# A block's output handed to the next block by single feature chunks, low halves one chunk behind

## The reference

```python
def rmsnorm(x, g):
    y = xf * lax.rsqrt(jnp.mean(xf * xf, axis=-1, keepdims=True) + RMS_EPS)
    return (y * g).astype(x.dtype)
# after each mixer and each network of the first block:
x = x + rmsnorm(y, g_post)          # y is the block's output
h = rmsnorm(x, g_pre)               # the next block's input
next_projection = h @ w             # 1024 features wide
```

## Time and profile before

| | us |
|---|---|
| median of 3 runs | 2015.49 |
| lowest and highest | 2012.11, 2020.97 |
| span of the profiled execution | 2011.9 |
| TensorE, VectorE, ScalarE, GpSimd busy in it | 1953.4, 1340.9, 1010.4, 320.4 |

### The profile page before, as it was taken

One profiled execution on the slowest core, in us unless ns is written; L12 is line 12 of the kernel. 1 busy time (PEld: TensorE's weight loads), 2 busy tenths in 40 slices (PEclk: granted clock), 3 DMA queues, 4 the chain that ended last, 5 costly groups with the idle time before them and its releaser, 6 DMA issues.

```text
span 2011.9 us, 34435 instructions
## 1 busy us (share of the span) xinstructions
PE 1953.4 (97%) x12338; PEld 1727.1 (86%) x12338; DVE 1340.9 (67%) x2732; ACT 1010.4 (50%) x1640; POOL 320.4 (16%) x138
## 2 busy tenths in 40 slices
PE   7998999999999999999999999999999999999998
PEld 6776787778778888999899999999999998888886
DVE  6357556656655558889787689933667766666666
ACT  5436546555554456666444455665444443333333
POOL 0000000000000000000000057877666600000000
PEclk9899999999989999999999999999999999999999
DMA  6242465533345553444343535555444455555554
GB/s 229 74 157 78 157 205 167 178 121 128 118 137 188 187 188 126 147 138 136 105 126 126 179 126 168 180 175 167 137 142 142 137 164 188 192 193 192 193 193 156
DMA packets 85150, 313.99 MB, mean 156 GB/s; under 512 B 9456, under 2 KB 9456, under 8 KB 84592
## 3 DMA queue, kind: packets, MB, share of 16 engines
q1 hardware_dynamic: 85040, 312.49, 46.6%
HBM read 311.40 MB, written 1.05 MB: 155 GB/s over the span
## 4 chain that ended last, share of the span: by engine, by line
issue 61%; PE 32%; POOL 6%; DVE 0%; POOLq 0%; DVEq 0%; ACT 0%
PE ps L414 17%; PE ps L282 12%; POOL wsplit L266 6%; PE ps L2642 3%; PE ps L430 0%; DVE work L2772 0%; DVE sq L2679 0%; POOLq L265 0%; PE ps L2718 0%; POOLq L2505 0%; DVE sq L2675 0%; DVE picks L2595 0%; PE ps L2608 0%; DVEq L2930 0%; DVE work L2687 0%
## 5 line engine op out<-in xcount | busy, mean ns | idle before, releaser
L260 ACT ACTIVATE wsplit<-ring 128x1024 fp32r<-128x1024 f32 x572 | 603.8, 1057 | 475.4 <-PE ps L414 270.4
L266 DVE TENSOR_TENSOR wsplit<-ring,wsplit 128x1024 fp32r<-128x1024 f32 x438 | 534.6, 1223 | 326.1 <-ACT wsplit L260 324.7
L282 PE MATMUL ps<-hsplit,wsplit 128*128 128x256 f32 x5064 | 646.2, 287 | 6.5 <-DVE hsplit L698 2.1
L282 PEld LDWEIGHTS ps<-hsplit,wsplit 128*128 128x128 f32 x5064 | 620.3, 193 | 14.3 <-issue 5.2
L266 POOL TENSOR_TENSOR wsplit<-ring,wsplit 128x1024 fp32r<-128x1024 f32 x134 | 320.2, 2396 | 1295.5 <-ACT wsplit L260 1295.5
L414 PE MATMUL ps<-wsplit,gsplit 128*128 128x512 f32 x1992 | 458.1, 391 | 0.0
L414 PEld LDWEIGHTS ps<-wsplit,gsplit 128*128 128x128 f32 x1992 | 374.4, 188 | 81.9 <-issue 4.2
L401 PE MATMUL ps<-wsplit,hsplit 128*128 128x512 f32 x1248 | 310.0, 406 | 17.2 <-DVE wsplit L266 10.6
L401 PEld LDWEIGHTS ps<-wsplit,hsplit 128*128 128x128 f32 x1248 | 241.9, 196 | 70.4 <-issue 18.9
L1783 PE MATMUL ps<-hsplit,wsplit 128*128 128x256 f32 x936 | 128.5, 289 | 0.0
L1783 PEld LDWEIGHTS ps<-hsplit,wsplit 128*128 128x128 f32 x936 | 116.3, 191 | 0.0
(11 more groups left out here) (318 smaller groups left out, 1698.5 us busy)
## 6 DMA issues: line engine op xcount, KB each, us to landing
ring<-in_weights SPq DMA_DIRECT2D x580, 512.0 KB, 3.3
work<-in_tables SPq DMA_DIRECT2D x1, 2123.0 KB, 12.5
xT<-in_x SPq DMA_DIRECT2D x1, 1024.0 KB, 4.9
work<-in_subkeys SPq DMA_DIRECT2D x1, 1024.0 KB, 15.2
work<-in_decay SPq DMA_DIRECT2D x2, 512.0 KB, 4.1
out_x<-work SPq DMA_DIRECT2D x2, 512.0 KB, 2.6
work<-in_w SPq DMA_DIRECT2D x1, 512.0 KB, 5.9
ring<-in_gain_row SPq DMA_DIRECT2D x1, 512.0 KB, 3.8
```

Of the source, the lines that this page charges most:

```text
L260: act.activation(wsplit[:, n % RING, 0, :], slab(s), ACT.Copy).then_inc(S("split", "lead"), 1)
L266: eng.tensor_tensor(wsplit[:, n % RING, 1, :], slab(s), wsplit[:, n % RING, 0, :], ALU.subtract).then_inc(S("split", RESTS[stream][0]), 1)
L282: mm = pe.matmul(dst, wsplit[:, n, a, c * P:(c + 1) * P], hsplit[:, b, c, :], start=(c == 0 and t == 0), stop=(c == KC - 1 and t == 2))
```

## The change

The three counters rise by one for each chunk. The add of every chunk signals, each leading half waits for its own chunk and signals, each low half waits for its own leading half and signals, and TensorE waits for one chunk's low half at a time. In the loop over chunks VectorE writes the low half of chunk c - 1 right behind the add of chunk c (before: a pair of low halves, one pair of adds behind), and the split of slab 1 stands behind the low half of chunk 1. `h_steps` works out the targets, since the inputs m0, m4 and m5 go on by pairs.

```diff
@@ split_project
             if pre is not None and c % 2 == 0:
-                wait_h_split(pe, pre, c // 2 + 1)
+                wait_h_split(pe, pre, c + 2)
@@
+    def h_steps(st, chunks):
+        whole = lambda s: KC if s[0] == "n" else KC // 2
+        return sum(whole(s) for s in HSPLITS[:HSPLITS.index(st)]) + (chunks if st[0] == "n" else chunks // 2)
@@ rest_h_vector
-        v.wait_ge(S("split", "h_lead"), HSPLITS.index(st) * 4 + c // 2 + 1)
+        v.wait_ge(S("split", "h_lead"), h_steps(st, c + 2))
@@
-    def wait_h_split(pe, st, steps=4):
-        pe.wait_ge(S("split", "h_rest"), HSPLITS.index(st) * 4 + steps)
+    def wait_h_split(pe, st, chunks=KC):
+        pe.wait_ge(S("split", "h_rest"), h_steps(st, chunks))
@@ split_columns
-        if pre is not None:
-            wait_h_split(pe, pre, q + 1)
         for cc in range(2):
             c = 2 * q + cc
+            if pre is not None:
+                wait_h_split(pe, pre, c + 1)
@@ ffn_tensor (moba_tensor and hgrn_tensor alike)
-        pe.wait_ge(S("norm", "x"), x_steps(POST[pre]) + 2)
+        pe.wait_ge(S("norm", "x"), x_steps(POST[pre]) + KC // 2)
@@ x_steps
-        return ROWS.index(st) * (KC // 2)
+        return ROWS.index(st) * KC
@@ rows_norm_vector, for c in range(KC):
-            ins = v.scalar_tensor_tensor(xT[:, c, :], YB[:, c, :], gain(g, c), xT[:, c, :], ALU.mult, ALU.add)
-            if c % 2:
-                ins.then_inc(S("norm", "x"), 1)
-                if late is not None and c > 1:
-                    late_rest_vector(v, late, c - 3)
-                if rests is not None and c == 3:
-                    rest_of(v, rests, 1)
+            v.scalar_tensor_tensor(xT[:, c, :], YB[:, c, :], gain(g, c), xT[:, c, :], ALU.mult, ALU.add).then_inc(S("norm", "x"), 1)
+            if late is not None and c > 0:
+                late_rest_vector(v, late, c - 1)
+            if rests is not None and c == 2:
+                rest_of(v, rests, 1)
         if late is not None:
-            late_rest_vector(v, late, KC - 2)
+            late_rest_vector(v, late, KC - 1)
@@ late_lead_scalar
-        else:
-            act.wait_ge(S("norm", "x"), x_steps(POST[st]) + c // 2 + 1)
         tokens_read(act, st, c)
         for k in range(c, c + 2):
-            ins = act.activation(hsplit[:, 0, k, :], xT[:, k, :], ACT.Copy, scale=gain(LATE_GAIN[st], k))
-        ins.then_inc(S("split", "h_lead"), 1)
+            if st not in ("n0", "n5"):
+                act.wait_ge(S("norm", "x"), x_steps(POST[st]) + k + 1)
+            act.activation(hsplit[:, 0, k, :], xT[:, k, :], ACT.Copy, scale=gain(LATE_GAIN[st], k)).then_inc(S("split", "h_lead"), 1)
@@
-    def late_rest_vector(v, st, c):
-        v.wait_ge(S("split", "h_lead"), HSPLITS.index(st) * 4 + c // 2 + 1)
+    def late_rest_vector(v, st, k):
+        v.wait_ge(S("split", "h_lead"), h_steps(st, k + 1))
+        v.scalar_tensor_tensor(hsplit[:, 1, k, :], xT[:, k, :], gain(LATE_GAIN[st], k), hsplit[:, 0, k, :],
+                               ALU.mult, ALU.subtract).then_inc(S("split", "h_rest"), 1)
+
+    def late_rests_vector(v, st, c):
         for k in range(c, c + 2):
-            ins = v.scalar_tensor_tensor(hsplit[:, 1, k, :], xT[:, k, :], gain(LATE_GAIN[st], k), hsplit[:, 0, k, :],
-                                         ALU.mult, ALU.subtract)
-        ins.then_inc(S("split", "h_rest"), 1)
+            late_rest_vector(v, st, k)
@@ late_norm_tensor
-        pe.wait_ge(S("norm", "x"), x_steps(POST[st]) + KC // 2)
+        pe.wait_ge(S("norm", "x"), x_steps(POST[st]) + KC)
@@ fox_vector and merge_vector (n0 and n5)
-        late_rest_vector(v, "n0", 0)
+        late_rests_vector(v, "n0", 0)
```

More of the change, by code:

```diff
@@ L1006, in fox_vector @@
     def fox_vector(v, own, st):
-        late_rest_vector(v, "n0", 0)
+        late_rests_vector(v, "n0", 0)
         rest_of(v, st, 0)
-        late_rest_vector(v, "n0", 2)
+        late_rests_vector(v, "n0", 2)
         rest_of(v, st, 1)
-        late_rest_vector(v, "n0", 4)
-        late_rest_vector(v, "n0", 6)
+        late_rests_vector(v, "n0", 4)
+        late_rests_vector(v, "n0", 6)
         rest_of(v, st, 2)
@@ L1090, in moba_tensor @@
     def moba_tensor(pe, st):
-        pe.wait_ge(S("norm", "x"), x_steps("p1") + 2)
+        pe.wait_ge(S("norm", "x"), x_steps("p1") + KC // 2)
         for g, bank in enumerate((4, 2)):
@@ L1865, in hgrn_tensor @@
     def hgrn_tensor(pe, st):
-        pe.wait_ge(S("norm", "x"), x_steps(POST["n4"]) + 2)
+        pe.wait_ge(S("norm", "x"), x_steps(POST["n4"]) + KC // 2)
         for q in range(4):
@@ L2396, in merge_vector @@
         merge_x_vector(v, st, KC - 4)
-        late_rest_vector(v, "n5", 0)
-        late_rest_vector(v, "n5", 2)
+        late_rests_vector(v, "n5", 0)
+        late_rests_vector(v, "n5", 2)
         merge_x_vector(v, st, KC - 2)
-        late_rest_vector(v, "n5", 4)
-        late_rest_vector(v, "n5", 6)
+        late_rests_vector(v, "n5", 4)
+        late_rests_vector(v, "n5", 6)
     def merge_x_vector(v, st, j):
```

## The result

| | runs | median us | lowest to highest |
|---|---|---|---|
| before | 16 | 2018.57 | 2012.11 to 2022.12 |
| after | 16 | 2022.18 | 2018.84 to 2026.03 |

The ratio is 1.0021, interval 1.0012 to 1.0030: 4.2 us slower (2.4 to 6.1), under half of the 0.5% that one set of runs can tell with ease, but clear of no change. The median of before came out 3 us higher in 16 runs than in the first three, so the forecast of 2020.2 us stood on a base that was low; its difference, +4.7 us, is what can be compared.

The account below looks back on a forecast made before the run. TensorE, busy 97% of the span, was taken to bound the kernel. Later starts of 4.5 us, less 1.4 and plus 1.6 for the clock, gave 4.7 us on 2015.5: 2020.2 us, range 2012.0 to 2026.5.

Parts of the forecast that it names:

- The order on VectorE: Stages p0 to p3: add 3 comes behind slab 1's split, so matmuls start 1.13 us later each, 4.5 us.
- The first matmul: Stages p0 to p3: starts at T + 4.00, before T + 2.87; T is the start of the first residual add.
- The clock: TensorE's low clock at the stage starts: 1.4 us given back, 1.6 us more for p1's longer low stretch.
- No new wait: TensorE's 25th matmul in a stage needs slab 2: taken as 0, bounds 0 to 0.4 us a stage.
- n0: The start of the program: first matmul at 10.59 still waits for slab 0, cost 0.
- n5: The pq stage: low 0 still ends 0.28 us behind GpSimd's subtraction, gain 0.
- more signals: Added signals on ScalarE, VectorE and the adds, and more TensorE waits: cost 0, bounds -0.1 to +0.2 us a stage.
- Faster: Rival, chance 0.08: first matmul needs low 0 alone and starts 1.18 us earlier, four times 4.7 us: 2010.8 us.
- Slower by more: Rival, chance 0.10: low clock lasts 3.4 us longer in all four stages, 10.9 us slower: 2026.4 us.
- The sum: Whole kernel: later starts 4.5 us, less 1.4 given back, plus 1.6 for p1's low stretch: 4.7 us slower.

Follow-up runs that it names:

- the second profile: The changed kernel measured again with nothing altered: ratio to before 1.0023 (2021.44 against 2017.68 us).
- the filled stand: Changed kernel plus three TensorE matmuls of constants behind the last transposes of each of p0 to p3: ratio to before 0.9999.
- the best start reached: Changed kernel with low halves two chunks behind the adds and slab 1 behind low half 1: ratio to before 0.9973, on another chip 0.9980.
- the slab twice: Changed kernel making the subtraction for slab 1 twice in a row ahead of add 3: ratio to before 1.0055 (2028.28 us).
- the three kernels' profiles with starts at T + 2.11: Changed kernel with low halves two chunks behind the adds, profiled twice (0.9973, 0.9980), and once with slab 2 also split earlier in p0 to p2 (0.9981).

## Why the prediction was right

*The order on VectorE.* Right, and shown as the cause. Add 3 was laid out at T + 3.38 and came at 3.39, low half 0 at 1.07 (1.06), low half 7 at 7.57 (7.60), slab 2 on ScalarE at 7.43 (7.47) and done on VectorE at 9.74 (9.77). Moving the split one place (ratio 1.0000), going back to the old order (0.9984) and doubling the split (1.0055) show it from both sides.

*The first matmul.* T + 4.00 was forecast, T + 3.92 came. The hand-over of 0.14 us was read from a low half; behind an add it is 0.05 to 0.06. The term is 1.04 to 1.05 us a stage instead of 1.13, 4.2 instead of 4.5 in all.

*The clock.* Two terms, 1.4 us given back and 1.6 us more for p1. The second held: p1's low stretch lasted 6.8 us instead of 3.4 in both profiles of the changed kernel. The first did not. It supposed that the low stretches stay where they are, and they moved: p0's began at T + 3.87 instead of 3.47 and p2's at T + 1.80 instead of 0.92, so the later starts took 0.1 and 0.2 us out of them where 0.5 and 1.1 were forecast. Together the terms were forecast at +0.2 us, and the low clock behind the first matmuls (15.9 against 14.7 us) makes them +0.6. Where the low stretches fall differs between executions of one kernel (19.3 us in the second profile, with 6.8 us in p0), so the size of these terms was not something to forecast to 1 us. That the stand brings on the low clock is shown by the filled stand. The rule of the Trainium skill cited ahead ("TensorE: Matmul & The Clock Gate", the section on what is actually happening), that activity releases the low level, agrees with it: with three matmuls of constants in the stand, the clock over p1's first 12 us was 1.00 instead of 0.72.

*No new wait, n0, n5, more signals.* All at nothing, as forecast: no wait for slab 2, the start at 10.58, the low half at n5 ending 0.28 us behind GpSimd. The reason given for slab 2, that every stage has a low stretch at its start, was needed: where one is missing, in p1 with the filled stand, the third slab starts about 0.45 us late, the upper bound that the term was given (0.4). The signals cost nothing that can be measured: with all of them and the split moved the ratio is 1.0000 (0.9989 to 1.0010), and four adds with a signal each take 1.66 us in the old order, as before.

*The rivals.* "Faster" was priced at T + 1.69 and would have needed the fourth add ahead of the split. With the fourth add ahead, the best start reached is T + 2.11, since the add itself takes VectorE's time; a gain of 4 to 5 us was there, in an order that the change did not have. "Slower by more" did not come. With the slab twice, low stretches of 6.8 us did come in all four stages, but with no more low clock behind the first matmuls than in the changed kernel: the later start takes the addition in.

*The sum.* +4.7 us forecast, +4.2 (2.4 to 6.1) measured. The main term was 0.3 us too large and the clock's 0.4 us too small, so that the sum comes this close is in part luck; the profile read by its stages gives 4.9.

## What to carry to other kernels

When a hand-over is made finer, list all that the waiting engine waits for, and put the last of these first on its producer: here the low half came 1.2 us earlier and the bank's release 2.2 us later, and only the later of the two counts. A long instruction (1.22 us among ones of 0.48) belongs behind the last thing that a standing engine needs. And where TensorE stands, count the low clock behind the stand as well as the stand.

## What the runs showed that was not expected

- A start 0.76 us earlier was worth 4 to 5 us over four stages where 3.1 was the sum at full clock, although a new wait for slab 2 took up to 2.6 us of it back. Fewer low stretches are the likely reason: from the first matmuls to T + 12 the three kernels' profiles with starts at T + 2.11 and no filled stand have 3.2, 8.9 and 10.3 us of low clock, before 14.7, the changed kernel 15.9 and 19.3. The numbers vary too much between profiles to show it.
- With the start at T + 2.11 slab 2 is the next limit: the third slab starts at T + 9.15 whether the first matmul starts at T + 2.11 or, with the filled stand in p0 and p2, at T + 2.81, and with no low clock ahead of it. So a still faster hand-over should win nothing more in p0 to p2 until slab 2 comes sooner (not tried).
- The low stretches ahead of p0, where the change touches n0 alone, differ by 17 us between two profiles (0.94 and 0.90 mean clock over 208 us), 8 us of time: a single span of this kernel says little about a change of 4 us, its waits and starts say it to the hundredth.
- A VectorE instruction issued while GpSimd's subtraction ran ended 0.28 us behind it whether it was issued 0.36 or 0.76 us into it.
